# Memory tiles scaled and split from a channels-first copy in SBUF, and the last four down pieces taken by row tile, in a two-layer fp32 encoder trunk

## The reference

```python
def reference(x, mem, ...):
    for i in range(DEPTH):                      # DEPTH = 2
        h = rmsnorm(x, g[0])
        x = x + rmsnorm(hybrid_mixer(h, ...), g[1])       # 16 heads, one output projection w_out
        mem_n = rmsnorm(mem, mem_norm[i])                 # mem: 256 x 2048, the same in both layers
        h = rmsnorm(x, g[2])
        x = x + rmsnorm(memory_xattn(h, mem_n, ...), g[3])
        h = rmsnorm(x, g[4])
        x = x + rmsnorm(conv_ffn(h, ...), g[5])           # ends with (gelu(gate) * val) @ w_down
    return x

def memory_xattn(h, mem_n, wq, wkv, wo):
    q = h @ wq
    k, v = split(mem_n @ wkv, 2)
    ...                                                   # 4 heads over the 256 memory tokens
```

## Time and profile before

| | |
|---|---|
| runs (3) | 2032.19, 2033.76, 2034.16 us; median 2033.76 |
| the profiled execution's own time | 2033.38 us |
| its span | 2031.6 us |
| mean granted TensorE clock | 0.991 of full speed |
| busy: PE, DVE, ACT, POOL | 1989.4, 1383.4, 1082.0, 168.0 us |
| moved by DMA | 367.68 MB, 181 GB/s |

### The profile page before, as it was taken

One profiled execution on the slowest core, in us unless ns is written; L12 is line 12 of the kernel. 1 busy time (PEld: TensorE's weight loads), 2 busy tenths in 40 slices (PEclk: granted clock), 3 DMA queues, 4 the chain that ended last, 5 costly groups with the idle time before them and its releaser, 6 DMA issues.

```text
span 2031.6 us, 30693 instructions
## 1 busy us (share of the span) xinstructions
PE 1989.4 (98%) x10772; PEld 1704.8 (84%) x10772; DVE 1383.4 (68%) x2154; ACT 1082.0 (53%) x1675; POOL 168.0 (8%) x191
## 2 busy tenths in 40 slices
PE   8999999998999999999999999999989999999997
PEld 7888888887888888888788888888878888888886
DVE  7757677857777777744567577768677777776444
ACT  6665556555555555444456654565555554554442
POOL 0010000000222121100000000000002222211000
PEclk9999999998999999999999999999989999999999
DMA  6564546544556665665535444665445655566662
GB/s 234 190 210 147 164 167 227 187 161 137 193 184 192 192 188 181 197 218 190 174 115 207 161 156 153 212 196 196 156 141 181 196 187 186 186 194 210 195 195 85
DMA packets 104959, 367.68 MB, mean 181 GB/s; under 512 B 12128, under 2 KB 13792, under 8 KB 103520
## 3 DMA queue, kind: packets, MB, share of 16 engines
q1 hardware_dynamic: 101872, 353.68, 53.7%
q10 hardware_dynamic: 2416, 11.14, 1.5%
q0 software_dynamic: 576, 1.57, 0.3%
HBM read 363.46 MB, written 2.88 MB: 180 GB/s over the span
## 4 chain that ended last, share of the span: by engine, by line
PE 91%; DVE 6%; ACT 2%; issue 1%; DMA 0%; SPq 0%; DVEq 0%; ACTq 0%
PE ps L788 24%; PE ps L726 13%; PE ps L728 12%; PE ps L727 12%; PE ps L791 12%; PE ps L738 9%; PE ps L741 4%; DVE w_lo L1412 1%; PE ps L690 1%; ACT w_hi L1081 1%; PE ps L1012 1%; PE ps L997 0%; DVE rtmp L1496 0%; PE ps L1000 0%; DVE x L1607 0%
## 5 line engine op out<-in xcount | busy, mean ns | idle before, releaser
L1412 DVE TENSOR_TENSOR w_lo<-raw,w_hi 128x1024 fp32r<-128x1024 f32 (+2 forms) x687 | 814.1, 1190 | 504.7 <-ACT w_hi L1081 500.0
L1081 ACT ACTIVATE w_hi<-raw 128x1024 fp32r<-128x1024 f32 (+2 forms) x687 | 704.7, 1031 | 486.9 <-PE ps L728 230.3
L788 PE MATMUL ps<-h_t,w_hi 128*128 128x512 f32 x2048 | 648.0, 398 | 2.4 <-DVE h_t L1429 2.4
L791 PEld LDWEIGHTS ps<-h_t,w_lo 128*128 128x128 f32 x2048 | 386.7, 189 | 91.9
L791 PE MATMUL ps<-h_t,w_lo 128*128 128x256 f32 x2048 | 403.8, 279 | 0.0
L788 PEld LDWEIGHTS ps<-h_t,w_hi 128*128 128x128 f32 x2048 | 313.5, 190 | 3.1 <-issue 3.1
L738 PE MATMUL ps<-h_t,w_hi 128*128 128x512 f32 x768 | 244.9, 400 | 0.1
L1963 POOL TENSOR_SCALAR up_c<-up_u,cw 128x256 f32<-128x256 f32 x128 | 125.8, 994 | 1176.8 <-DVE up_u L1858 1176.8
L726 PE MATMUL ps<-w_hi,act_t 128*128 128x512 f32 x512 | 199.2, 389 | 0.0
L727 PE MATMUL ps<-w_lo,act_t 128*128 128x512 f32 x512 | 199.2, 389 | 0.0
L728 PE MATMUL ps<-w_hi,act_t 128*128 128x512 f32 x512 | 199.2, 389 | 0.0
(11 more groups left out here) (301 smaller groups left out, 2277.7 us busy)
## 6 DMA issues: line engine op xcount, KB each, us to landing
raw<-stream SPq DMA_DIRECT2D x639, 512.0 KB, 3.9
raw<-stream SPq DMA_DIRECT2D x24, 288.0 KB, 2.9
raw<-stream SPq DMA_DIRECT2D x16, 262.0 KB, 3.0
gain_a<-gains_in ACTq DMA_DIRECT2D x4, 1024.0 KB, 6.6
m_nat<-mem_in ACTq DMA_DIRECT2D x2, 2048.0 KB, 10.1
gain_f<-gains_in ACTq DMA_DIRECT2D x2, 1024.0 KB, 8.0
out<-x SPq DMA_DIRECT2D x8, 256.0 KB, 2.8
x<-x_in SPq DMA_DIRECT2D x3, 512.0 KB, 8.6
```

Source lines behind the costliest of these rows:

```text
L788: pe.matmul(ps[:, 4 * half + nt, :], hi[:, cc, nt * P:(nt + 1) * P], h_t[:, c, :, :], start=(c == 0), stop=False, skip_group_check=True)
L791: mm = pe.matmul(ps[:, 4 * half + nt, SEQ:2 * SEQ], lo[:, cc, nt * P:(nt + 1) * P], h_t[:, c, 0, :], start=False, stop=(c == KC - 1), skip ...
L1081: act.activation(w_hi[:, slot, 0:width], raw[:, rslot, 0:width], ACT.Copy).then_inc(hi_ready, 1)
L1412: dve.tensor_tensor(w_lo[:, slot, 0:width], raw[:, rslot, 0:width], w_hi[:, slot, 0:width].bitcast(F32), ALU.subtract).then_inc(lo_ready, 1)
```

## The change

Four things:

1. The host also hands over the memory as `mem_t_in`, channels-first: 128 partitions x 16 chunks x 256 rows, 16 KB in a row for each partition. `load_mem` loads it into `m_x` (same place, same wait, 2 MB). The step `mem_T` leaves PE: ACT writes hi from `m_x`, DVE lo from `m_x`, with semaphores of their own (`mem_hi`, `mem_tile`), and the kind leaves `BANKED` and `TSPLITTED`.
2. `m_nat` is loaded, squared and turned into a root in layer 0 only. It now lies at 80 K, the place of `h_t` and `m_t`. Its load is a step of its own, `load_mem_rows` at `P_OUT + 2`, and `mem_stats` 1 stands at `P_OUT + 17` instead of `+ 18`. `("R", "mem")` and the copy to `rm_t` stay in both layers.
3. In layer 0 hi tiles wait until both sums of squares are read (`mem_sq` 2), as `m_t` takes the place of `m_nat`.
4. In the last layer the last four down pieces, 12 to 15, are taken by row tile instead of the last two.

```diff
@@ layer_steps
     for i in range(8):
         at(P_OUT + 18 + i, ("mem_T", i))
-    at(P_OUT + 16, ("mem_stats", 0))
-    at(P_OUT + 18, ("mem_stats", 1))
-    at(P_OUT + 20, ("mem_rstd",))
+    if layer == 0:
+        at(P_OUT + 2, ("load_mem_rows",))
+        at(P_OUT + 16, ("mem_stats", 0))
+        at(P_OUT + 17, ("mem_stats", 1))
+        at(P_OUT + 20, ("mem_rstd",))
     at(P_OUT + 22, ("R", "mem"))
@@
+LAST_BY_TILE = 16 - SPL
@@ build
-        m_nat = sb("m_nat", [P, TB, D], BIG + 48 * K)
+        m_nat = sb("m_nat", [P, TB, D], 80 * K)
+        m_x = sb("m_x", [P, KC, SEQ], BIG + 48 * K)
@@ PE, the piece that reads m_t
                         for t in range(2):
-                            tile_ready((tiles, 2 * j + t))
+                            if tiles == "mem_T":
+                                pe.wait_ge(mem_tile, l * 8 + (2 * j + t + 1))
+                            else:
+                                tile_ready((tiles, 2 * j + t))
@@ PE, steps
-                    elif kind == "mem_T":
-                        i = step[1]
-                        pe.wait_ge(mem_here, l * 16 + 16)
-                        b = take_bank(step)
-                        for kk in range(2):
-                            for tb in range(TB):
-                                mm = pe.transpose(b[:, kk * SEQ + tb * P:kk * SEQ + (tb + 1) * P],
-                                                  m_nat[:, tb, (2 * i + kk) * P:(2 * i + kk + 1) * P], ident[:])
-                        mm.then_inc(bank_done, 1)
@@ PE, down projection
-                    for j in range(16 if k < 3 else 14):
+                    for j in range(16 if k < 3 else 14 if l < DEPTH - 1 else LAST_BY_TILE):
...
-                        for j in (14, 15):
+                        for j in range(LAST_BY_TILE, 16):
@@ ACT, steps
                     elif kind == "load_mem":
                         act.wait_ge(*item_done(l, ("head_T", 7)))
+                        act.dma_start(m_x[:], mem_t_in).then_inc(mem_x_here, 16)
+                    elif kind == "load_mem_rows":
+                        act.wait_ge(*pieces_used(l, P_OUT))
                         act.dma_start(m_nat[:], mem_in.rearrange("(t p) d -> p t d", p=P)).then_inc(mem_here, 16)
+                    elif kind == "mem_T":
+                        i = step[1]
+                        act.wait_ge(*pieces_used(l, P_OUT))
+                        act.wait_ge(mem_sq, 2)
+                        act.wait_ge(mem_x_here, l * 16 + 16)
+                        dst, chunks, gains = tsplit_job(step, l)
+                        for kk, c in enumerate(chunks):
+                            ins = act.activation(dst[:, c, 0, :], m_x[:, c, :], ACT.Copy, scale=gains[kk])
+                        ins.then_inc(mem_hi, 1)
@@ DVE, steps
+                    elif kind == "mem_T":
+                        dve.wait_ge(mem_hi, l * 8 + step[1] + 1)
+                        c = 2 * step[1]
+                        lo_tile(*tsplit_job(step, l), m_x[:, c:c + 2, :].rearrange("p c s -> p (c s)")).then_inc(mem_tile, 1)
@@ host
+              "mem_t_in": w["mem"].reshape(SEQ, KC, P).transpose(2, 1, 0),
```

More of the change, by code:

```diff
@@ L306, in piece_width @@
     return ch * w
-BANKED = ("latent_T", "latent_qk_T", "head_T", "O", "T", "forget_scan", "R", "mem_T", "h1", "h1_0", "h1_1", "h2", "h3", "XS", "XT", "XO", "bias")
+BANKED = ("latent_T", "latent_qk_T", "head_T", "O", "T", "forget_scan", "R", "h1", "h1_0", "h1_1", "h2", "h3", "XS", "XT", "XO", "bias")
 def bank_items():
@@ L346 @@
 LATENT_CHUNKS = [[0, 1], [2], [3], [4], [5]]
-TSPLITTED = ("latent_T", "head_T", "mem_T", "h1", "h1_0", "h1_1", "h2", "h3", "XO")
+TSPLITTED = ("latent_T", "head_T", "h1", "h1_0", "h1_1", "h2", "h3", "XO")
 TSPLIT = {key: n for n, key in enumerate(k for k in ITEM if k[1][0] in TSPLITTED)}
@@ L360, in done, with build @@
         self.eng.wait_ge(self.sem, self.n)
-def build(nc, stream, x_in, mem_in, pos_in, consts_in, cols_in, rows_in, lam_in, gains_in, out):
+def build(nc, stream, x_in, mem_in, mem_t_in, pos_in, consts_in, cols_in, rows_in, lam_in, gains_in, out):
     with ExitStack() as ctx:
@@ L530, in build @@
         mem_here = sem("mem_here")
+        mem_x_here = sem("mem_x_here")
+        mem_hi = sem("mem_hi")
+        mem_tile = sem("mem_tile")
         first_here = sem("first_here")
@@ L911, in _ @@
                         if step[1] == "mem":
-                            pe.wait_ge(rstm_ready, l + 1)
+                            pe.wait_ge(rstm_ready, 1)
                         else:
@@ L1208, in _ @@
                         if gi == G_MEMV:
-                            act.wait_ge(rstm_ready, l + 1)
+                            act.wait_ge(rstm_ready, 1)
                             act.wait_ge(memv_first, l + 1)
@@ L1308, in _ @@
                         act.wait_ge(*item_done(l, ("head_T", 7)))
+                        act.dma_start(m_x[:], mem_t_in).then_inc(mem_x_here, 16)
+                    elif kind == "load_mem_rows":
+                        act.wait_ge(*pieces_used(l, P_OUT))
                         act.dma_start(m_nat[:], mem_in.rearrange("(t p) d -> p t d", p=P)).then_inc(mem_here, 16)
+                    elif kind == "mem_T":
[7 more added lines that the diff above has]
+                        ins.then_inc(mem_hi, 1)
                     elif kind == "mem_stats":
                         tb = step[1]
-                        act.wait_ge(mem_here, l * 16 + 16)
+                        act.wait_ge(mem_here, 16)
                         act.wait_ge(y_sq, l * 24 + 4)
                         if tb == 1:
-                            act.wait_ge(mem_sq, l * 2 + 1)
+                            act.wait_ge(mem_sq, 1)
                         act.activation(junk[:], m_nat[:, tb, :], ACT.Square, accum_out=ssq[:, tb:tb + 1]).then_inc(mem_sq, 1)
@@ L1691, in _ @@
                         dve.sem_inc(rstx_ready, 1)
+                    elif kind == "mem_T":
+                        dve.wait_ge(mem_hi, l * 8 + step[1] + 1)
+                        c = 2 * step[1]
+                        lo_tile(*tsplit_job(step, l), m_x[:, c:c + 2, :].rearrange("p c s -> p (c s)")).then_inc(mem_tile, 1)
                     elif kind == "mem_rstd":
-                        dve.wait_ge(mem_sq, l * 2 + 2)
+                        dve.wait_ge(mem_sq, 2)
                         rsqrt(rst_m[:], 8, 8 + TB, [(ssq[:, 0:TB], D, TB)])
```

## The result

The changed kernel takes **2022.78 us** (median of 6 runs, 2020.12 to 2023.87) beside 2033.96 us for the kernel before in the same session (6 runs, 2032.19 to 2035.08). The ratio is 0.9942, 95% interval 0.9932 to 0.9952: by it 11.8 us faster, between 9.8 and 13.8. The two medians themselves lie 11.2 us apart, the two means 11.4. The forecast was 10.4 us, with at most 11.6 inside the range.

What follows compares the result with a forecast made beforehand. PE, busy 98% of the span, was taken to bound the kernel; 7.7 us from the transposes plus 2.7 at the end make 10.4 off 2033.76, so 2023.4 us, range 2022.2 to 2026.0.

Steps and rivals of the forecast that it cites:

- The transposes: Output projection of the mixer: taking the memory's transposes off PE saves 3.84 us in layer 0, 3.82 in layer 1, 7.7 together.
- R alone at 0.50: Spreading of the root on PE stays in the output projection; standing alone it was left 0.45 + 0.05 = 0.50 us.
- ACT and DVE keep up: Output projection: per piece with a mem step ACT needs 1.68 us and DVE 1.94 of PE's 2.72.
- the walk: Layer 0's ACT and DVE work followed in order against PE's pieces: nothing of PE's waits, 2.2 us of cover for R.
- The loads: m_x lands well before its first hi tile, 11.5 us of cover; the additional 2 MB rows' load in layer 0 costs 0.
- the rival's working: Rival "m_x lands late", 1%: ACT waits before mem_T 0; PE idles, lacking piece +22, once the load takes over 26.6 us.
- The end: Last down pieces: four by row tile let DVE go from row tile 0 to 1 without a gap, 2.7 us gone.
- brings nothing by itself: Layer 1 without squares (2 x 1.90 us on ACT) and root (2.64 on DVE): no gain, since PE did not wait.
- The sum: Whole kernel: 7.7 us from the output projection plus 2.7 from the end, 10.4 us.
- so no clock is to be won: Stretches where the memory is transposed: PEclk is 1.00, the upper level (2.4 GHz), so no gain from the clock.
- the low end: Lower edge of the range, 2022.2 us, a little below the forecast case's 2022.4; a median can sit 1 us off.
- more than forecast: Rival for the whole kernel: R's share goes too and runs fall low, 2022.0 us; 4%.

Runs made afterwards that it cites:

- The late load: The changed kernel with the load of m_x issued behind piece +17 of the output projection instead of +11: 2024.87 us, ratio 0.9958.
- The padded kernel: The changed kernel with DVE repeating the root's small instructions in layer 1 on scratch columns nobody reads, without row load or squares: 2023.55 us, ratio 0.9948.

## Why the prediction came out as it did

*The transposes: right.* Priced by distances at 3.84 and 3.82 us, measured 3.85 in both layers by DVE's distances (3.86 by PE's), and the same again when put back alone. The durations (17.4 us) would have been wrong by more than twice. R alone at 0.50 follows from it. The two starts of layer 1 in the earlier trace rows lie half a piece, 1.36 us, ahead of the pieces that they were named for; that nine pieces with all extras lie between them holds.

*ACT and DVE keep up: right*, and by the walk: 2.4 us of cover for R where 2.2 stood, no wait of PE between +18 and +31 in either layer. The tiles last 494 and 479 ns against 493 and 480 taken. By the rule of the Trainium skill (Perfetto Trace Analysis, Optimizing Scalar/DVE Operations) ACT's tile should be 42 ns longer from SBUF and DVE's 65 shorter, in the time that the engine is busy with it. For ACT the trace agrees nearly: a pair of tiles keeps it 0.80 us instead of 0.73, 35 ns a tile, though the durations differ by only 494 - 473 = 21. For DVE it doesn't: the durations are 479 and 478, and two tiles take 0.79 us from SBUF where they took 0.80. Neither touched the time.

*The loads: right.* m_x landed in 8.9 us, the rows in 11.0 us at 322 GB/s beside a PE that stayed busy 10.00 of 10. The late load showed that the wait would cost 0.8 us when the load is issued 16 us later, and that the rival's working was off: the first thing that PE lacks is the root for R and not piece +22, 2 us of load time before the 26.6 named.

*The end: right to 0.3 us.* 2.7 forecast; 2.7 where the end is changed alone, 2.41 in the changed kernel, which has the pause in front of y_f that the kernel before has not, and 2.7 again (181.66 to 178.92) between two kernels that both have it.

*The root in layer 1 "brings nothing by itself": nearly.* By PE's waits it is true; through DVE's pause it brings 0.36 us in layer 1 and costs 0.3 at the end.

*The sum: right by distances*, 10.5 against 10.4. The measured 11.8 has 1.3 us more and the 11.96 over all runs 1.5, and this is where the prediction failed: the low-clock time outside the edited stretches is a term that it put at nothing. The step is in its second paragraph: PEclk is 1.00 in the stretches that are edited, "so no clock is to be won". I read the clock only where the edit was. The same page has an 8 in PEclk's line in two slices, at the ends of the memory sub-layers, and the low stretches there, some 27 us in all of the profiled execution, take 2.0 us less on the mean of four profiles of the changed kernel, of which slower first loads took 0.9 back. The other half of the failure is the width: the low end allowed 1 us for a median sitting off, while single runs of the changed kernel lie 4 us apart (2019.87 to 2023.95) and those of the kernel before in that session 3. A low end 2 us below the forecast, half of the wider scatter, would have been 2021.4. On which side of the range's end the result came to lie, by 0.2 us, is luck; that 10.4 is short of 11.96 +- 0.62 is not. The rival "more than forecast" had 4% for a reason (R's share and runs that fall low) of which only the second half has support.

*Open:* why the changed kernel's runs hold less low-clock time. The kernel with the transposes put back is 8.6 +- 0.9 us slower than the changed one. The 8.9 of its expectation, by which the excess hangs on how close the layers lie, is well inside these bounds; the 7.7 by which it doesn't is at their edge, and the 7.4 of the distances outside. So most of the excess seems to go with the transposes. The padded kernel has the same transposes gone and leaves 0.3 over, so the transposes gone are not enough by themselves, as far as four runs can tell. In all four profiles of the changed kernel the clock falls late, 4.55 to 4.73 us after PE's stop, in layer 1; which part of the change brings that about is not shown.

## What to carry to other kernels

On an engine that never idles, price what is taken away by the distance between its neighbours with and without it, not by its duration: here 64 x 272 ns were worth 7.7 us and not 17.4, and the estimate held to 0.04 us a layer. What lies on engines with room to spare may be dropped or kept with little effect: here 3.8 us of ACT and 2.6 of DVE moved the time by a third of a microsecond. And before giving a range, read the granted clock over the whole span, not only in the edited stretch: a stretch at half clock elsewhere may change from run to run by more than a small part of the edit is worth.

## What was not expected of the hardware

- **A pause of DVE that moves when twelve of its instructions come or go.** 0.35 us in front of y_a in layer 1 (0.77 instead of 0.42) or 0.29 us in front of y_f at the end, with no semaphore to explain it. Twelve instructions that nobody reads put the pause back at y_a and took it away from y_f. It came out the same in all profiles of the same program; its cause is not shown.
- **The time at the lower clock around the same idle time is not fixed.** PE is idle for 5.3 us at the end of the memory sub-layer in every profile. The clock falls in that time, and stays at 1.2 GHz for 10.2 us where it fell 2.0 to 4.4 us after PE stopped, and for 6.8 us where it fell 4.55 to 5.0 us after; both occur in one program. In the turn the second stretch of 3.4 us is there or is not, and with it 1.5 us of the time (100.5 or 99.0).
- **Transposes among matmuls did not lower the clock.** With 32 of 272 ns in 26 us of layer 0 PEclk is 1.00, as it is without them.
